# The rotation's partner rows in the third mixer: from a TensorE permutation to DMAs between partitions

## The reference, cut to what matters

```
q = _partial_rope(_rmsnorm(q, q_norm), cos, sin)
k = _partial_rope(_rmsnorm(k, k_norm), cos, sin)

def _partial_rope(x, cos, sin):
    half = ROT_DIM // 2                       # ROT_DIM = 16
    x1, x2, rest = xf[..., :half], xf[..., half:ROT_DIM], xf[..., ROT_DIM:]
    return concatenate([x1 * c - x2 * s, x2 * c + x1 * s, rest])
```

## Time and profile before

| | us |
|---|---|
| median of three runs | 1782.19 (1781.84 to 1782.19) |
| profiled execution | 1783.92 |
| span of its trace | 1782.0 |
| PE busy | 1734.2 (97%) |
| DVE busy | 1153.4 (65%) |
| ACT busy | 1128.9 (63%) |
| POOL busy | 1230.5 (69%) |

### The profile page before, as it was taken

One profiled execution on the slowest core, in us unless ns is written; L12 is line 12 of the kernel. 1 busy time (PEld: TensorE's weight loads), 2 busy tenths in 40 slices (PEclk: granted clock), 3 DMA queues, 4 the chain that ended last, 5 costly groups with the idle time before them and its releaser, 6 DMA issues.

```text
span 1782.0 us, 27146 instructions
## 1 busy us (share of the span) xinstructions
PE 1734.2 (97%) x9776; PEld 1044.7 (59%) x9776; DVE 1153.4 (65%) x1873; ACT 1128.9 (63%) x1581; POOL 1230.5 (69%) x1788
## 2 busy tenths in 40 slices
PE   7989999999999999999999999999999999999999
PEld 3546666655555556666666666666655555566665
DVE  6885777138888755777127857775257777577720
ACT  8887666455977667666454977665543544866641
POOL 7847777876555557777866657778765454677785
PEclk9999999999999999999999999999999999999999
DMA  7323444545222225444533014444432222344453
GB/s 266 110 95 120 152 146 144 161 151 162 72 95 95 95 83 172 148 151 139 162 128 109 34 50 146 148 149 154 153 119 95 86 96 72 107 154 142 148 156 122
DMA packets 65613, 226.56 MB, mean 127 GB/s; under 512 B 8149, under 2 KB 9173, under 8 KB 64981
## 3 DMA queue, kind: packets, MB, share of 16 engines
q1 hardware_dynamic: 64236, 221.88, 38.6%
q10 hardware_dynamic: 1245, 2.95, 0.5%
HBM read 222.51 MB, written 2.10 MB: 126 GB/s over the span
## 4 chain that ended last, share of the span: by engine, by line
PE 74%; DVE 12%; ACT 8%; issue 4%; DMA 1%; POOL 1%; SPq 0%; ACTq 0%; DVEq 0%; POOLq 0%
PE psum L295 22%; PE psum L305 21%; PE psum L337 12%; PE psum L341 11%; ACT w_big L250 1%; DMA y_rest<-in_ssd_tables 1%; DVE psum L1621 1%; DVE arena L2018 1%; PE psum L2236 1%; ACT psum L1468 1%; DVE arena L2016 1%; PE psum L2271 1%; PE psum L1833 1%; DVE psum L1706 1%; ACT L1501 1%
## 5 line engine op out<-in xcount | busy, mean ns | idle before, releaser
L266 POOL TENSOR_TENSOR w_rest<-w_panel,w_big 128x256 bf16<-128x256 f32 x1660 | 1166.7, 741 | 467.8 <-ACT w_big L250 467.8
L295 PE MATMUL psum<-x_big,w_big 128*128 128x512 f32 x2248 | 655.4, 424 | 8.7 <-ACT x_big L387 6.6
L305 PE MATMUL psum<-x_rest,w_rest 128*128 128x512 bf16 x2248 | 555.8, 382 | 1.7 <-DVE x_rest L483 1.7
L250 ACT ACTIVATE w_big<-w_panel 128x1024 fp32r<-128x1024 f32 (+1 forms) x415 | 418.3, 1032 | 171.7 <-PE psum L341 99.9
L295 PEld LDWEIGHTS psum<-x_big,w_big 128*128 128x128 f32 x2248 | 415.3, 189 | 136.1 <-issue 26.7
L305 PEld LDWEIGHTS psum<-x_rest,w_rest 128*128 128x128 bf16 x2248 | 188.6, 98 | 283.3 <-issue 102.8
L701 DVE SCALAR_TENSOR_TENSOR psum<-ffn_raw,params,psum 128x512 f32<-128x512 f32 x352 | 264.6, 752 | 7.2 <-ACT psum L655 1.0
L693 DVE TENSOR_TENSOR ffn_raw<-psum,rstd 128x512 f32<-128x512 f32 x176 | 121.3, 691 | 139.0 <-PE psum L305 121.3
L655 ACT ACTIVATE psum<-ffn_raw,params 128x512 f32<-128x512 f32 x176 | 137.4, 782 | 102.0 <-DVE ffn_raw L693 101.7
L337 PE MATMUL psum<-g_big,w_big 128*128 128x512 f32 x704 | 199.3, 423 | 0.0
L547 DVE SCALAR_TENSOR_TENSOR x_resid<-psum,x_resid 128x512 f32<-128x512 f32 x64 | 43.8, 689 | 225.0 <-PE psum L341 216.9
(11 more groups left out here) (263 smaller groups left out, 1728.0 us busy)
## 6 DMA issues: line engine op xcount, KB each, us to landing
w_panel<-in_up SPq DMA_DIRECT2D x176, 512.0 KB, 3.5
w_panel<-in_dn SPq DMA_DIRECT2D x64, 448.0 KB, 3.2
w_panel<-in_ssd_in SPq DMA_DIRECT2D x41, 512.0 KB, 3.3
w_panel<-in_dn SPq DMA_DIRECT2D x32, 512.0 KB, 3.5
w_panel<-in_hgrn_in SPq DMA_DIRECT2D x32, 512.0 KB, 3.3
w_panel<-in_lru_in SPq DMA_DIRECT2D x18, 512.0 KB, 3.5
w_panel<-in_ssd_out SPq DMA_DIRECT2D x16, 512.0 KB, 3.3
w_panel<-in_swa_in SPq DMA_DIRECT2D x12, 512.0 KB, 3.3
```

The costliest lines, as they stand in the source:

```text
L250: act.activation(k.w1[:, slot, 0:words], k.w[:, slot, 0:words], ACT.Copy, scale=(SHIFT - 1) / SHIFT).then_inc(k.s("panel_big"), 1)
L266: rest = pool.tensor_tensor(k.w2[:, slot, a], k.w[:, slot, a], k.w1[:, slot, a].bitcast(F32), ALU.subtract)
L295: pe.matmul(out, k.w1[:, slot, q * m:(q + 1) * m], k.x1[:, q, :], start=q == 0, stop=False)
L305: mm = pe.matmul(out, k.w2[:, slot, q * m:(q + 1) * m], k.x2[:, q, :], start=False, stop=q == DT - 1)
```

## The change

PE no longer multiplies by the permutation. SP copies the partner rows instead, with four DMAs for each of the ten tiles (two heads, two halves, 8 partitions of 512 floats, 16 KB each) into one of two buffers in SBUF that take turns; the buffers are zeroed once by DVE. The four DMAs of tile i stand in SP's queue behind the load of panel i+7 (those of k tile 0 with tile 4's, of k tile 1 with tile 5's), wait for the eviction of the tile (or the k norm) and for the release of the buffer. The second product of the rotation reads SBUF alone. The norm's weights, which the permutation held, are now in two sine tables (one for q, one for k), with the partners' weights as parameters. `normed` moves from slot 5 to slot 4. A semaphore of the second mixer is merged into another.

```
-SWA_TABLE = P + P + 3 * 256 + 2 * S
+SWA_TABLE = P + 3 * 256 + 2 * S
+        self.partner = self.pt[:, 0, :, :]
+        self.cos_q, self.cos_k, self.sin_q, self.sin_k = (a.take(S) for _ in range(4))
+SWA_AHEAD = 7
-        if slot == 5:
+        if slot == 4:
             ev += [("normed", 0, 0), ("normed", 1, 0)]
-        if i in (1, 5, 6):
+        if i == 1:
             in_big(pe, k, job, i)
-            norm_tensor(pe, k, 4) if i == 1 else rope(i - 5, 0)
+            norm_tensor(pe, k, 4)
-    def rope(i, _):
-        ...
-        pe.matmul(k.ps[:, 4, :], b.perm_k if i < 2 else b.perm_q, b.tile(i), start=True, stop=True
-                  ).then_inc(k.s("swa_partner"), 1)
+def swa_sync(sp, k, i):
+    b, half = SwaBuffers(k), ROT // 2
+    for tile in ((i - 4, i) if i in (4, 5) else (i,) if 2 <= i < SWA_V else ()):
+        n = rope_index(tile)
+        if tile < 2:
+            sp.wait_ge(k.s("swa_normed"), tile + 1)
+        else:
+            sp.wait_ge(k.s("banks_free"), k.evicted("swa_in", tile))
+        if n >= 2:
+            sp.wait_ge(k.s("swa_rotated"), 3 * n - 4)
+        else:
+            sp.wait_ge(k.s("swa_setup"), 5)
+        for to in (0, 64):
+            for at in (0, half):
+                sp.dma_start(b.partner[to + at:to + at + half, n % 2], b.tile(tile)[to + half - at:to + ROT - at]
+                             ).then_inc(k.s(f"swa_partner{n % 2}"), 16)
 def swa_vector(dve, k):
+    dve.memset(b.partner, 0.0).then_inc(k.s("swa_setup"), 1)
     dve.wait_ge(k.s("mixer_landed"), 112)
-    for cos, perm, g in ((b.cos_k, b.perm_k, k.p("swa_k_norm")), (b.cos_q, b.perm_q, k.p("swa_q_norm"))):
-        dve.tensor_scalar(cos, b.cos, g, None, ALU.mult).then_inc(k.s("swa_setup"), 1)
-        dve.tensor_scalar(perm, b.perm, g, None, ALU.mult).then_inc(k.s("swa_setup"), 1)
+    for cos, sin, part in ((b.cos_k, b.sin_k, "swa_k"), (b.cos_q, b.sin_q, "swa_q")):
+        dve.tensor_scalar(cos, b.cos, k.p(part + "_norm"), None, ALU.mult).then_inc(k.s("swa_setup"), 1)
+        dve.tensor_scalar(sin, b.sin, k.p(part + "_partner"), None, ALU.mult).then_inc(k.s("swa_setup"), 1)
@@ rotation on DVE
-        dve.wait_ge(k.s("swa_partner"), n + 1)
-        dve.tensor_tensor(b.xs, k.ps[:, 4, :], b.sin, ALU.mult).then_inc(k.s("swa_rotated"), 1)
+        dve.wait_ge(k.s(f"swa_partner{n % 2}"), 64 * (n // 2 + 1))
+        dve.tensor_tensor(b.xs, b.partner[:, n % 2], b.sin_k if i < 2 else b.sin_q, ALU.mult).then_inc(k.s("swa_rotated"), 1)
@@ SP's loop over the panels
                 weights_sync(sp, k, n)
+                swa_sync(sp, k, n - k.panel0["swa_in"] - SWA_AHEAD)
```

More of the change, by code:

```diff
@@ L1293, in turn @@
             if g == 0:
-                pe.wait_ge(k.s("ssd_decays"), 2)
+                pe.wait_ge(k.s("ssd_decays"), 3)
                 pe.wait_ge(k.s("ssd_dt_t"), 3)
@@ L1449, in dt @@
             return
-        act.activation(b.ea, k.p("ssd_a_log"), ACT.Exp).then_inc(k.s("ssd_ea"), 1)
+        act.activation(b.ea, k.p("ssd_a_log"), ACT.Exp).then_inc(k.s("ssd_decays"), 1)
         act.wait_ge(k.s("banks_free"), k.evicted("ssd_in", 0))
@@ L1576, in dt @@
             softplus_join(dve, softplus, b.size, b.q, b.dt)
-            dve.wait_ge(k.s("ssd_ea"), 1)
+            dve.wait_ge(k.s("ssd_decays"), 1)
             dve.wait_ge(k.s("ssd_ones"), 16)
@@ L1588, in decays @@
         if part == 2:
-            dve.wait_ge(k.s("ssd_decays"), 2)
+            dve.wait_ge(k.s("ssd_decays"), 3)
             dve.tensor_tensor(b.dt_end.rearrange("p c h -> p (c h)"), k.ps[:, 5, P:2 * P],
@@ L2076 @@
 ROPE_THETA = 500000.0
-SWA_TABLE = P + P + 3 * 256 + 2 * S
+SWA_TABLE = P + 3 * 256 + 2 * S
+SWA_PARTNER = np.arange(64)
+SWA_PARTNER[0:ROT] = (SWA_PARTNER[0:ROT] + ROT // 2) % ROT
 class SwaBuffers:
@@ L2092, in __init__ @@
         self.pt = a.take(2, 2, 4 * P)
-        self.cos_q, self.cos_k = a.take(S), a.take(S)
-        self.perm_q, self.perm_k = a.take(P), a.take(P)
+        self.partner = self.pt[:, 0, :, :]
+        self.cos_q, self.cos_k, self.sin_q, self.sin_k = (a.take(S) for _ in range(4))
         self.fq = a.take(64)
@@ L2099, in __init__ @@
         self.table = t
-        self.half_mean, self.perm = t[:, 0:P], t[:, P:2 * P]
-        self.mask = t[:, 2 * P:2 * P + 768]
-        self.cos, self.sin = t[:, 1024:1024 + S], t[:, 1024 + S:1024 + 2 * S]
+        self.half_mean, self.mask = t[:, 0:P], t[:, P:P + 768]
+        self.cos, self.sin = t[:, P + 768:P + 768 + S], t[:, P + 768 + S:SWA_TABLE]
     def tile(self, i):
@@ L2278, in early @@
         out_steps(pe, k, "swa_out", o, t, t + 1, k.y1, k.y2)
-    do = {"tile": tile_, "mean": mean, "turn_v": turn_v, "stat": stat, "rope": rope, "score": score, "turn": turn,
-          "pv": pv, "early": early}
+    do = {"tile": tile_, "mean": mean, "turn_v": turn_v, "stat": stat, "score": score, "turn": turn, "pv": pv,
+          "early": early}
     for what, i, o in swa_events():
@@ L2375, in rope @@
         x = b.tile(i)
-        dve.wait_ge(k.s("swa_setup"), 4)
+        dve.wait_ge(k.s("swa_setup"), 5)
         if i < 2:
@@ L2643, in swa_table @@
     i = np.arange(P)
[L2644 to L2648, removed]
     key = np.arange(256)
@@ L2660, in swa_table @@
     half = (i[:, None] // 64 == i // 64) / 64
-    return np.concatenate([half, perm, *masks, cos, sin], axis=1).astype(np.float32)
+    return np.concatenate([half, *masks, cos, sin], axis=1).astype(np.float32)
 def hgrn_masks():
@@ L2694, in layout @@
         "swa_q_norm": np.tile(a["swa_q_norm"][0], 2)[:, None], "swa_k_norm": np.tile(a["swa_k_norm"][0], 2)[:, None],
+        "swa_q_partner": np.tile(a["swa_q_norm"][0][SWA_PARTNER], 2)[:, None],
+        "swa_k_partner": np.tile(a["swa_k_norm"][0][SWA_PARTNER], 2)[:, None],
         "swa_sinks": np.tile(a["swa_sinks"][0], (P, 1)),
```

2 lines of the change are left out of this document (1 added, 1 removed).

## The result

| | before | after |
|---|---|---|
| median of 18 runs each | 1781.89 (1781.15 to 1782.38) | 1785.05 (1783.56 to 1787.00) |
| ratio, 95% interval | | 1.0018 (1.0011 to 1.0025) |
| profiled execution; span | 1783.92; 1782.0 | 1784.01; 1782.2 |
| mean granted clock of PE | 1.000 | 0.997 (0.996 in 8 of the 18 runs) |

A forecast was written before the change was run, and what follows sets the result against it. PE was taken to bound the kernel, with DVE nearly as late around 943 to 957. Of at most 10.9 us, 2.1 by unit 0's maximum plus ACT's vanished wait gave 2.7: 1782.19 - 2.7 = 1779.5 us, range 1777.0 to 1783.4.

The forecast's parts named there:

- tile 6's statistic to tile 9: Third mixer: after PE's idle wait, two pairs fewer gain 1.9 us, so tile 9 is evicted at 971.1, not 973.06.
- PE's clock falls: Rival, chance 0.09: PE's clock drops in the idle gap before tile 6's statistic, costing about 2.5 us; total 1782.0.
- the late rows: Rival, chance 0.20: partner-row copies issue or land late; gain falls to 1.8 or 1.0, or the kernel gets slower.
- First second-product: Tile 2's rotation on DVE: four copies issued by 939.4, landing 1.9 us later, so DVE begins at 941.3.
- Sixteen operations in SBUF at 0.98: DVE's work from 941.3 to tile 6's eviction: 16 x 0.98 plus 1.2 for two evictions, 16.9 us.
- The rival of the lighter chain: Rival, chance 0.25: more DVE operations run beside an idle POOL, at 0.8 each; gain 4.3 us, 1777.9.
- Copies for k tile 1 "just in time": SP's tightest copies, behind panel 12's load, land at 955.5; DVE comes there at about 956.
- Tile 6 at 958.2: DVE evicts tile 6 of the third mixer at 958.2, 1.2 us later than before.
- PE idle about 4 with ACT as releaser: PE stands idle about 4 us before tile 6's statistic, until ACT's logarithm; PE goes on at about 962.2.
- Memset and sine tables hidden: DVE's head grows by 1.4 us (memset 1.0, sine tables 0.4), covered by 1.77 us of idle time.
- Merged semaphore 0: Second mixer: the merged semaphore orders what was in order already, cost 0.
- SBUF products beside POOL: Second products now reading SBUF cost 0.98 us in place of 0.68, the slower class beside POOL's splits.

The follow-up runs named there:

- e1: Changed kernel plus 20 unread matmuls on PE ahead of the wait of tile 6's statistic; 1782.55 us, ratio 1.0003.
- e10: Changed kernel plus unread matmuls ahead of the statistics of tiles 4 to 6 and eight transposes ahead of the second mixer's table wait; 1782.70 us, ratio 1.0003.
- e15: e10 with the parameters and the third mixer's table at their old sizes in DRAM; ratio 0.9991.
- e2: Changed kernel plus 5, 6 and 20 unread matmuls ahead of the statistics of tiles 4, 5 and 6; 1783.72 us, ratio 1.0009.
- e8: Changed kernel with copies one panel earlier, plus 6 and 17 unread matmuls ahead of the statistics of tiles 5 and 6; 1779.48 us, ratio 0.9986.
- e14: Changed kernel without the 40 copies and DVE's waits for them, so the rotation is missing from the result; 1782.76 us, ratio 0.9996.
- e5: Kernel before with only the second mixer's semaphore merged into another; 1782.11 us, ratio 0.9999.
- e6: Changed kernel with copies one panel earlier and the statistics of tiles 6 to 9 in PSUM bank 4; 1778.29 us, ratio 0.9981.
- e3: Changed kernel with copies issued one panel earlier; 1781.52 us, ratio 0.9997.
- e13: Changed kernel with the parameters and the third mixer's table at their old sizes in DRAM; ratio 1.0007.
- e4: Changed kernel with the statistics of tiles 6 to 9 in PSUM bank 4, so tile 6's needn't wait for the logarithm; 1783.15 us, ratio 1.0004.
- e11: e6 plus 5 and 4 unread matmuls ahead of the statistics of tiles 5 and 6; 1779.17 us, ratio 0.9981.
- e12: e11 plus eight unread transposes ahead of the second mixer's wait for its table; 1778.47 us, ratio 0.9976.

## Why the prediction was wrong

The step that failed is the one from tile 6's statistic to tile 9. The forecast put PE idle for 4 us and then ran everything behind at full pace: tile 9 at 971.1, nothing for the clock in the sum. The clock fell instead, and tile 9 came at 975.17. The prediction had this as its rival "PE's clock falls", with a chance of 0.09. It is what happened, in all 18 runs: none has a mean clock above 0.997, where the kernel before had 1.000 in every run beside an experiment. The rival's price of 2.5 us was right: the fill gives 2.7 back by ratio and 2.4 in the stretch. The trace of before had no gap between 1.6 and 6.4 us, so 0.09 rested on nothing.

The clock alone does not make up the miss. From -2.7 to +3.2 there are 5.9 us, and the rival with its price would have ended at 1782.0, unchanged. In the stretch the account closes: forecast -2.7; tile 6 is 0.8 later than forecast and the gain behind it smaller, which leaves -1.5 with the clock held (e1, 228.13 against 229.60); and the fallen clock adds 2.4, which gives the +0.9 measured. The other 2.3 us of the 3.2 lie outside the stretch or in the executions with a lower clock; the second mixer has 0.4 of them in after's profile, and 1.0 on the means. The rest stays open.

By ratios the split is, with an uncertainty of about 2 us on each term: clock 2.7 us (after to e10, 1.0018 to 1.0003), sizes in DRAM 2.1 us by the ratios but 0.9 by the second mixer's length (e10 to e15), and what is left of the change with both put right, -1.6 us (e15, 0.9991; interval -3.2 to 0). These add up to +3.2 by construction, as each term is a difference of two neighbours. The forecast's -2.7 stands against that last term; by the stretch 841 to 1071 it is 227.62 - 229.60 = -2.0 (e15). That still holds the late rows, which by e2 and e8 are worth 2.9 us of the stretch.

Point by point:
- First second-product: forecast 941.3, is 941.77. Right, by luck: an issue takes 0.67 and not the 0.47 chosen (0.6 us up to the fourth), and the mixer starts 0.4 earlier.
- Sixteen operations in SBUF at 0.98: from 941.77 to 958.66 less 1.7 of waits and 1.2 of evictions are 14.0, 0.87 each. The rival of the lighter chain was half true and by luck paid for the next point.
- Copies for k tile 1 "just in time" (955.5): they land at 956.95, and DVE waits 1.44 us. The load in front of them is issued at 952.44 where 951.9 was forecast, and four issues take 2.7 us, not 1.9. Without copies tile 6 is evicted 2.1 us earlier (e14).
- Tile 6 at 958.2: is 958.66, so near only because the stretch starts 0.4 earlier; the delay is 2.1 us and not 1.2. PE idle about 4 with ACT as releaser: 4.66, right.
- Tile 9 at 971.1: is 975.17, the failed step.
- Memset and sine tables hidden: the memset takes 0.91, and DVE still has 0.99 us idle before the first eviction (1.77 before). Right.
- Merged semaphore 0: right (e5). "Costs nothing" overlooked the sizes of the two tensors, which no view of before shows as a cost.
- SBUF products beside POOL: the new second product takes 0.68 at 947.01, where POOL waits for ACT, and 0.86 (949.83) and 1.07 (956.95) beside a split. At 941.77 it takes 0.69, though POOL is in a split from 941.13 on, so not every such operation is slowed. The Trainium skill ("SBUF — State Buffer", "Who interferes with whom") says that a DVE instruction with two SBUF inputs contends with a GpSimd instruction that reads SBUF; the trace agrees, but for the one at 941.77.

## What to carry to other kernels

Taking matmuls out of PE's queue where another engine is nearly as late turns busy time into idle time in front of a wait, and PE's clock can then fall: price the gap at both clock levels before counting the gain, and look at the granted clock first. Removing the reasons for the wait (a bank that isn't shared and copies issued one panel earlier, together 6.6 us by ratio, after to e6) was worth more than filling it (2.7). A profiled execution is one sample: e6's was the slowest of eleven, and an expectation built on its clock failed. Compare whole runs by ratio on one chip: here two profiled executions differed by 0.1 us where the medians differed by 3.2.

## What was not expected of the hardware

- The length of a gap alone does not decide over the clock. In the third mixer it fell to its lower level in or behind every gap of 3.8 to 4.8 us (after, e3, e13, e14), but also after 1.05 (after) and 1.21 (e6), while 1.44 six us ahead of the latter did nothing, nor did 1.98 in e4 and before's 1.22. In the second mixer it fell behind a wait of 2.04 (e2) and held behind 2.37 (e8). The same wait near 986 to 990 went both ways: of 1.82 us, a fall in e11 and none in e12; of 1.35, a fall in e10 and none in e1. What else decides stays open. The Trainium skill ("TensorE: Matmul & The Clock Gate", "HAM oscillation — how this bites in real kernels") ties the fall to longer idle gaps; the trace agrees for the long ones and not for those of about 1 us.
- Behind the gaps in front of a statistic stand eight matmuls of two columns each, behind those at 414 and 990 other ones. The clock fell behind both kinds; the work behind a gap was not varied alone.
- A DMA of eight rows of 2 KB between partitions takes as long to issue (0.67 us) as two panels of 512 KB (0.33 each).
- 64 KB less in one tensor of DRAM and 1 KB more in another go with later panels (7.6 to 8.3 us instead of 6.1 to 7.4) in a mixer that uses neither of the changed parts, and with 1.0 us more for that mixer. Either size alone does not show it.
